# First stage of a transformer kernel: four row pieces, halved weight loads on two queues, and a later transpose

## The chip, the cores and the metric

The kernel runs on one core of one Trainium2 chip. The metric is the device time of one execution in microseconds (us), lower is better. A core has TensorE (PE, with its weight loads PEld), VectorE (DVE), ScalarE (ACT), GpSimd (POOL) and SyncE (SP); SP and ACT issue transfers here, each through a queue of its own (q1 is SP's, q10 is ACT's), and 16 DMA engines carry both.

## What is computed

The reference is a model of two blocks over 256 tokens of width 1024. Only the beginning of the first block matters here, the input product of the mLSTM mixer:

```
def mlstm_mixer(x, w_in, b_ig, b_fg, head_g, w_out):
    B, S, _ = x.shape
    proj = x @ w_in
    q, k, v, o, ig, fg = jnp.split(proj, M_SPLITS, axis=-1)
...
```

x is 256 x 1024 in float32 and w_in is 1024 x 3080. Everything else (the recurrent cell, attention, feed-forward layers, the second block) comes after this product.

## The kernel before

**Precision.** A float32 product is made of three matmuls on rounded parts. For the weights, ACT writes the high part `wh` from the landed float32 weights (`split_half_high`, L314) and DVE writes the low part `wl`, the difference (`split_half_low`, L324). For the rows, TensorE turns 128x128 tiles of x into PSUM (L3321), ACT copies the high part `xT_high` (L3444), DVE the low part `xT_low` (L3542). The products are high rows by high weights (wh,xT_high), low rows by high weights (wh,xT_low), and high rows by low weights (wl,xT_high).

**Tiling.** x has eight tiles of 128 columns; two neighbours form a *pair*, and the step `xturn pair` turns the four 128x128 blocks of one pair (two tiles, two groups of 128 rows). The weights come as numbered *loads* into a ring of four slots of 2048 columns. Loads 0 and 1 are the first 392 columns of w_in (in two strips, 8 columns and 384 columns), for the first and the last four tiles of x; loads 2 and 3 are the next 512 columns. Each load is split into a half 0 (two tiles) and a half 1. I write half (1,0) for half 0 of load 1.

**Order.** The first stage has one hand-written list, `steps()`. TensorE, ACT and DVE each walk the whole list in order and issue their own part of each step. So a step's place in the list fixes its place in three instruction streams, and each of these engines takes its stream in order. `dense c, half, t, ks` is TensorE's product for column group c, load 2c + half, row group t and tiles ks; `high n, j` is ACT's split and `low n, j` DVE's. An `xturn` is TensorE's four transposes, then ACT's copy of `xT_high`, then DVE's `xT_low`. In the dense step of c = 0, t = 0 the three kinds of product are taken in the order in which their operands come (L3284 wh,xT_high; L3287 wh,xT_low; L3290 wl,xT_high), each with its own wait; the step for t = 1 follows at L341 to L343. The list begins:

```
        yield "xturn", 0
        yield "high", 0, 0
        yield "low", 0, 0
        yield "xturn", 1
        yield "high", 0, 1
        yield "dense", 0, 0, 0, range(2)
        yield "dense", 0, 0, 1, range(2)
        yield "low", 0, 1
        yield "xturn", 2
        yield "xturn", 3
        yield "dense", 0, 0, 0, range(2, 4)
        yield "dense", 0, 0, 1, range(2, 4)
        yield "high", 1, 0
        yield "low", 1, 0
```

**Transfers.** ACT issues half (0,0) (L3437: 8 KB, then 384 KB). SP issues the left half of x (pairs 0 and 1, 512 KB), half (0,1) (8 and 384 KB), the right half of x, load 1 whole (16 and 768 KB), loads 2 and 3 (1024 KB each), and then many small vectors. While the first rows are under way TensorE does four matmuls on ones (L3265), and five short ones after pair 0 (L3326); their results are not used.

Of the kernel before, what the change touches and what calls it, by code (L numbers as in the profile page):

```python
# [27 lines left out]
P = 128  # L28
SEQ = 256
TT = SEQ // P  # L30
D = 1024
KT = D // P
BANK = 512
# [23 lines left out]
SLOTS = 4  # L57
# [163 lines left out]
def parts_of(K, n):  # L221

    if K.slot_of[n] is None:
        return K.early_high[:, :], K.early_low[:, :]
    return K.wh[:, K.slot_of[n], :], K.wl[:, K.slot_of[n], :]
# [14 lines left out]
def joined(slot, k, width):  # L240
    return slot[:, 0:k * width].rearrange("p (k n) -> p k n", k=k)


def pieces_in(K, n, slot):

    out, at = [], 0
    if isinstance(K.loads[n], Joined):
        whole = joined(slot, K.loads[n][0].shape[1], sum(p.shape[2] for p in K.loads[n]))
        for src in K.loads[n]:
            out.append(whole[:, :, at:at + src.shape[2]])  # L250
            at += src.shape[2]
        return out
    for src in K.loads[n]:
        k, w = src.shape[1], src.shape[2]
        out.append(slot[:, at:at + k * w].rearrange("p (k n) -> p k n", k=k))
        at += k * w
    return out
# [8 lines left out]
def load_weights(K, sp, n):  # L266

    if n < len(K.loads):
        for dst, src in zip(pieces_in(K, n, K.ring[:, n % SLOTS, :]), K.loads[n]):
            sp.dma_start(dst, src).then_inc(K.slot_loaded[n % SLOTS], 16)  # L270


def load_size(K, n):
    return sum(p.shape[1] * p.shape[2] for p in K.loads[n])
# [22 lines left out]
def half_of(w, j):  # L297

    if w <= SLOT * 3 // 4:
        return (0, w) if j == 1 else None  # L300
    return (j * w // 2, (j + 1) * w // 2)


def split_half_high(K, act, n, j):

    if n < len(K.loads) and half_of(load_size(K, n), j):
        lo, hi = half_of(load_size(K, n), j)
        if n == 0 and j == 0:
            act.wait_ge(K.first_loaded, 16 * len(K.loads[0]))
        elif n == 0 or lo == 0:  # L310
            act.wait_ge(K.slot_loaded[n % SLOTS], 16 * sum(len(K.loads[m]) for m in range(n % SLOTS, n + 1, SLOTS)))
            if K.part_after[n] is not None:
                act.wait_ge(K.load_used, K.part_after[n] + 1)
        K.nc.scalar.activation(parts_of(K, n)[0][:, lo:hi], K.ring[:, n % SLOTS, lo:hi], ACT.Copy).then_inc(  # L314
            K.high_ready, 2 if lo == 0 and j == 1 else 1)
# [42 lines left out]
def refill(K, sp, first, count):  # L358

    for n in range(first + AHEAD, first + AHEAD + count):  # L360
        if n < len(K.loads):
            sp.wait_ge(K.low_ready, 2 * n + 2)
            load_weights(K, sp, n + SLOTS)
# [331 lines left out]
class Tail:  # L695
# [121 lines left out]
    def act(self, act, own=None):  # L817

        K, nc = self.K, self.K.nc
        for step, *args in self.order():  # L820
            if step == "square":
                t, h = args
                s = slice(h * BANK, (h + 1) * BANK)
                self.rows(act, t, h)
                nc.scalar.activation(K.hid_flat[:, t, s], K.x[:, t, s], ACT.Square,
                                     accum_out=K.stat[:, t, h:h + 1]).then_inc(K.square_ready.sem, 1)
            elif step == "high":
                t, h = args
                act.wait_ge(K.turned.sem, self.turned0 + 2 * t + h + 1)
                for first, n in self.tiles(h):  # L830
                    m = nc.scalar.activation(K.xT[0][:, first:first + n, t * P:(t + 1) * P],
                                             self.bank(t, h, first, n), ACT.Copy, scale=self.scale(first))
                m.then_inc(K.high_turned.sem, 1)
            elif step == "lead_high":
                i, j = args
                if i == 0 and j == 0 and self.region:
                    act.wait_ge(*self.region)
                split_half_high(K, act, self.lead_load + i, j)
            elif own:
                own(step, *args)  # L840
# [470 lines left out]
def load_rows(K, sp, which):  # L1311

    for r, vec in which.items():
        w = vec.shape[0]
        sp.dma_start(K.rows[:, r, 0:w], vec.partition_broadcast(P)).then_inc(K.row_loaded[r], 16)
# [748 lines left out]
def nsa_mixer(K, a, tail):  # L2064
# [657 lines left out]
    def _(act):  # L2722
        for step, *args in steps():
            if step == "high":
                split_half_high(K, act, first + args[0], args[1])
            elif step == "take" and args[1] == 0:
                c, _ = args
# [292 lines left out]
def mlstm_mixer(K, a, tail):  # L3020
# [41 lines left out]
    def steps():  # L3062
# [7 lines left out]
        yield "dense", 0, 0, 1, range(2)  # L3070
        yield "low", 0, 1
        yield "xturn", 2
        yield "xturn", 3
        yield "dense", 0, 0, 0, range(2, 4)
        yield "dense", 0, 0, 1, range(2, 4)
        yield "high", 1, 0
        yield "low", 1, 0
        yield "high", 1, 1
        yield "low", 1, 1
# [151 lines left out]
    @block.sync  # L3231
    def _(sp):
        x_rows = a["x"][0].rearrange("(t p) d -> p t d", p=P)
        sp.dma_start(K.x[:, :, 0:BANK], x_rows[:, :, 0:BANK]).then_inc(K.input_loaded, 16)
        for dst, src in zip(pieces_in(K, 0, K.ring[:, 0, :]), K.loads[0]):
            sp.dma_start(dst[:, 2:4, :], src[:, 2:4, :]).then_inc(K.slot_loaded[0], 16)
        sp.dma_start(K.x[:, :, BANK:D], x_rows[:, :, BANK:D]).then_inc(K.rest_loaded, 16)
        for n in range(1, SLOTS):
            load_weights(K, sp, n)
        sp.dma_start(K.gate_bias[0:M_HEADS, 0:1], a["a_b_igate"][0].unsqueeze(1)).then_inc(K.bias_loaded, 16)  # L3240
        sp.dma_start(K.gate_bias[0:M_HEADS, 1:2], a["a_b_fgate"][0].unsqueeze(1)).then_inc(K.bias_loaded, 16)
        sp.dma_start(K.positions[:, :], a["positions"][0].rearrange("(t p) -> p t", p=P),
                      allow_slow_non_contiguous=True).then_inc(K.small_loaded, 16)
        for name, vec in lists:
            c, m = K.col_of[name], vec.shape[0] // P
            sp.dma_start(K.z[c:c + m, 0, 0:P], vec.rearrange("(k p) -> k p", p=P)).then_inc(K.small_loaded, 16)
        sp.dma_start(K.gate_bias[0:FOX, 2:3], a["b_forget_2"][0].unsqueeze(1)).then_inc(K.small_loaded, 16)
        sp.dma_start(K.sinks[:, :], a["b_sinks"][0].partition_broadcast(P)).then_inc(K.small_loaded, 16)
        refill(K, sp, first - AHEAD, 1)
        for i, name in enumerate(["q_norm_nsa_2", "k_norm_slc_2", "k_norm_win_2", "q_norm_fox_2", "k_norm_fox_2",  # L3250
                                  "k_norm_cmp_2"]):
            sp.dma_start(K.head_gain[:, i, :], a[name][0].partition_broadcast(P)).then_inc(K.small_loaded, 16)
        refill(K, sp, first - AHEAD + 1, 2)
        load_rows(K, sp, {0: a["mix_ln_g"][0], 1: a["mix_ln_b"][0]})
        refill(K, sp, first - AHEAD + 3, 11)
        sp.wait_ge(K.scores_ready.sem, H)
        load_rows(K, sp, {2: a["mlp_ln_g"][0], 3: a["mlp_ln_b"][0]})
        given.sp(sp)
        refill(K, sp, first - AHEAD + 14, 6)

    @block.tensor
    def _(pe):
        pe.wait_ge(K.ones_ready, 1)
        for i in range(4):
            nc.tensor.matmul(K.psum[:, 0, 0:SEQ], K.ones[:, 0:P], K.ones[:, :], start=True, stop=True)  # L3265
        for step, *args in steps():
            if step == "dense":
                c, half, t, ks = args
                n = first + 2 * c + half
# [40 lines left out]
                    mm.then_inc(K.filled.sem, 1)  # L3310
            elif step == "xturn":
                pair, = args
                if pair == 0:
                    pe.wait_ge(K.input_loaded, 16)
                    pe.wait_ge(K.masked, 1)
                elif pair == 2:
                    pe.wait_ge(K.rest_loaded, 16)
                for j in range(2):
                    for t in range(TT):
                        kk = 2 * pair + j  # L3320
# [113 lines left out]
    def _(act):  # L3434
        G = K.gates
        for dst, src in zip(pieces_in(K, 0, K.ring[:, 0, :]), K.loads[0]):
            act.dma_start(dst[:, 0:2, :], src[:, 0:2, :]).then_inc(K.first_loaded, 16)  # L3437
        for step, *args in steps():
            if step == "high":
                split_half_high(K, act, first + args[0], args[1])  # L3440
            elif step == "xturn":
                pair, = args
# [501 lines left out]
def build(nc, a, out):  # L3944
    K = Kit()
    K.nc = nc
    with ExitStack() as ctx:
# [3 lines left out]
        def sem(name):  # L3951
            return ctx.enter_context(nc.semaphore(name))
# [208 lines left out]
        K.high_ready = sem("high_ready")  # L4161
        K.low_ready = sem("low_ready")
        K.load_used = sem("load_used")
        K.input_loaded = sem("input_loaded")
        K.rest_loaded = sem("rest_loaded")
        K.first_loaded = sem("first_loaded")
        K.small_loaded = sem("small_loaded")
        K.bias_loaded = sem("bias_loaded")
        K.zeroed = sem("zeroed")
# [97 lines left out]
```

## Time and profile before

| | |
|---|---|
| median of 3 runs | 1200.76 us (1200.52 to 1201.33) |
| the profiled execution | 1200.72 us, of which span 1199.0 us |
| TensorE busy | 1186.3 us (99% of the span) |
| VectorE busy | 747.1 us (62%) |
| ScalarE busy | 618.9 us (52%) |
| bytes moved | 210.80 MB, mean 176 GB/s |

TensorE is busy almost without a gap. What matters is therefore the few places where it waits, and whether an edit makes one shorter or adds one. All of the edited code runs in the first 20 us of the span. In a row of the timeline, `x4` counts instructions merged into one row, and the square brackets hold how long the engine had been idle and what released it. A matmul's row on PE begins when its data streams; the weight load (PEld) of the same matmul begins somewhat earlier, and PEld rows are the better clock for "when did TensorE get here".

### The profile page before, as it was taken

To read this page: it belongs to the slowest core of one execution; us is meant where nothing else is said; L and a number is where in the kernel's file an instruction comes from. 1 tells how busy PE (TensorE), PEld (TensorE's weight loads), DVE (VectorE), ACT (ScalarE), POOL (GpSimd) and SP (SyncE) were. 2 spreads that over 40 slices of the span, in tenths; PEclk is the share of its full clock that TensorE was granted. 3 is DMA by queue.
4 is the path that set the end of the run, shared out by engine and by line. 5 is a ranking of instruction groups with operands and counts; after the bars stand their busy time and mean duration, and the time that the engine had idled before them with its cause. 6 is when DMAs were issued, how large, how long until landed. Compare 5 with 4: busy or idle time off the path is not lost.

```text
span 1199.0 us, 16307 instructions
## 1 busy us (share of the span) xinstructions
PE 1186.3 (99%) x6455; PEld 1009.3 (84%) x6455; DVE 747.1 (62%) x990; ACT 618.9 (52%) x924; POOL 42.5 (4%) x64
## 2 busy tenths in 40 slices
PE   9999999999999999999999999999999999999998
PEld 8888899898777789999888888888878788888887
DVE  6769655556865774554697455448986465554447
ACT  5464544344465544444456434436886674444445
POOL 2000000000000000000000000001111010000001
PEclk9999999999999999999999999999999999999999
DMA  8655554654753356556545565554651336655540
GB/s 292 209 188 207 194 194 163 206 197 153 228 180 111 115 210 198 189 177 202 184 145 187 194 209 178 182 171 144 192 166 69 115 124 210 195 191 171 180 176 36
DMA packets 119964, 210.80 MB, mean 176 GB/s; under 512 B 8320, under 2 KB 67024, under 8 KB 119888
## 3 DMA queue, kind: packets, MB, share of 16 engines
q1 hardware_dynamic: 119344, 209.35, 52.6%
q8 instruction: 52, 0.85, 0.3%
q10 hardware_dynamic: 544, 0.40, 0.1%
q14 instruction: 24, 0.20, 0.1%
HBM read 208.68 MB, written 1.05 MB: 175 GB/s over the span
## 4 chain that ended last, share of the span: by engine, by line
PE 90%; DVE 6%; ACT 2%; issue 1%; DMA 0%; POOL 0%; ACTq 0%; DVEq 0%; POOLq 0%
PE psum L341 23%; PE psum L343 23%; PE psum L342 23%; PE psum L349 4%; PE psum L355 3%; PE psum L350 3%; PE psum L1431 2%; PE psum L1399 2%; DVE wl L324 1%; PE psum L1418 1%; PE psum L853 1%; PE psum L540 1%; DVE early_low L324 1%; DVE bn L775 1%; DMA ring<-in_a_w_in 0%
## 5 line engine op out<-in xcount | busy, mean ns | idle before, releaser
L293 DVE TENSOR_TENSOR wl<-ring,wh 128x2048 fp32r<-128x2048 f32 x131 | 300.0, 2292 | 263.3 <-ACT wh L284 263.2
L284 ACT ACTIVATE wh<-ring 128x2048 fp32r<-128x2048 f32 x131 | 250.6, 1915 | 215.0 <-PE psum L343 215.0
L341 PE MATMUL psum<-wh,xT_high 128*128 128x512 f32 (+4 forms) x576 | 225.0, 391 | 0.0
L343 PE MATMUL psum<-wh,xT_low 128*128 128x512 f32 (+4 forms) x576 | 218.8, 380 | 0.0
L342 PE MATMUL psum<-wl,xT_high 128*128 128x512 f32 (+4 forms) x576 | 218.1, 379 | 0.0
L341 PE MATMUL psum<-wh,hidT_high 128*128 128x512 f32 (+2 forms) x472 | 178.8, 380 | 0.2
L342 PE MATMUL psum<-wl,hidT_high 128*128 128x512 f32 (+2 forms) x472 | 178.0, 379 | 0.0
L343 PE MATMUL psum<-wh,hidT_low 128*128 128x512 f32 (+2 forms) x472 | 177.9, 378 | 0.0
L341 PE MATMUL psum<-xT_high,wh 128*128 128x256 f32 x480 | 136.0, 283 | 0.0
L343 PE MATMUL psum<-xT_high,wl 128*128 128x256 f32 x480 | 135.8, 283 | 0.0
L342 PE MATMUL psum<-xT_low,wh 128*128 128x256 f32 x480 | 135.8, 283 | 0.0
L324 DVE TENSOR_TENSOR wl<-ring,wh 128x1024 fp32r<-128x1024 f32 (+4 forms) x101 | 120.8, 1214 | 11.5 <-ACT wh L314 10.9
L341 PEld LDWEIGHTS psum<-wh,xT_high 128*128 128x128 f32 x576 | 108.3, 188 | 20.5 <-issue 2.0
L343 PEld LDWEIGHTS psum<-wh,xT_low 128*128 128x128 f32 x576 | 108.3, 188 | 20.6
L342 PEld LDWEIGHTS psum<-wl,xT_high 128*128 128x128 f32 x576 | 108.5, 188 | 18.2
L314 ACT ACTIVATE wh<-ring 128x1024 fp32r<-128x1024 f32 (+4 forms) x101 | 103.2, 1057 | 34.6 <-PE psum L343 22.0
L341 PEld LDWEIGHTS psum<-wh,hidT_high 128*128 128x128 f32 (+2 forms) x472 | 85.3, 181 | 18.1 <-issue 1.4
L343 PEld LDWEIGHTS psum<-wh,hidT_low 128*128 128x128 f32 (+2 forms) x472 | 85.2, 181 | 17.4
L342 PEld LDWEIGHTS psum<-wl,hidT_high 128*128 128x128 f32 (+2 forms) x472 | 85.3, 181 | 16.6
L341 PEld LDWEIGHTS psum<-xT_high,wh 128*128 128x128 f32 x480 | 92.0, 192 | 0.6
L342 PEld LDWEIGHTS psum<-xT_low,wh 128*128 128x128 f32 x480 | 92.0, 192 | 0.6
L343 PEld LDWEIGHTS psum<-xT_high,wl 128*128 128x128 f32 x480 | 92.0, 192 | 0.0
(325 smaller groups left out, 1477.9 us busy)
## 6 DMA issues: line engine op xcount, KB each, us to landing
ring<-in_mlp_w_up SPq DMA_DIRECT2D x32, 1024.0 KB, 5.7
ring<-in_mlp_w_down SPq DMA_DIRECT2D x32, 1024.0 KB, 5.0
ring<-in_ffn_wg SPq DMA_DIRECT2D x44, 512.0 KB, 4.0
ring<-in_ffn_wu SPq DMA_DIRECT2D x44, 512.0 KB, 5.0
ring<-in_ffn_wd SPq DMA_DIRECT2D x22, 1024.0 KB, 5.0
ring<-in_ple_w_gate SPq DMA_DIRECT2D x12, 1024.0 KB, 5.1
ring<-in_w_in SPq DMA_DIRECT2D x10, 1024.0 KB, 5.1
ring<-in_a_w_in SPq DMA_DIRECT2D x8, 1024.0 KB, 10.5
```

What stands on the lines that cost most here:

```text
L284: K.nc.scalar.activation(parts_of(K, n)[0][:, 0:w], K.ring[:, n % SLOTS, 0:w], ACT.Copy).then_inc(K.high_ready, 2)
L293: K.nc.vector.tensor_tensor(low[:, 0:w], K.ring[:, n % SLOTS, 0:w], high[:, 0:w].bitcast(F32), ALU.subtract).then_inc(K.low_ready, 2)
L314: K.nc.scalar.activation(parts_of(K, n)[0][:, lo:hi], K.ring[:, n % SLOTS, lo:hi], ACT.Copy).then_inc(K.high_ready, 2 if lo == 0 and j == ...
L324: K.nc.vector.tensor_tensor(low[:, lo:hi], K.ring[:, n % SLOTS, lo:hi], high[:, lo:hi].bitcast(F32), ALU.subtract).then_inc(K.low_ready, 2 ...
L341: nc.tensor.matmul(out, x[0], w[0], start=start, stop=False)
L342: nc.tensor.matmul(out, x[0], w[1], start=False, stop=False)
L343: return nc.tensor.matmul(out, x[1], w[0], start=False, stop=stop)
L349: nc.tensor.matmul(out, x[0], w[0], start=start, stop=False)
L350: nc.tensor.matmul(out, x[0], w[1], start=False, stop=False)
L355: return K.nc.tensor.matmul(out, x[1], w[0], start=False, stop=stop)
L1399: nc.tensor.matmul(out, u["q"], u["k"], start=True, stop=False)
L1431: mm = nc.tensor.matmul(K.psum[:, self.value_bank, at:at + HD], self.probsT[:, i % 2, (2 * a + j) * P:(2 * a + j + 1) * P], u["v"][a][j], ...
```

## The change

x comes in four pieces of 256 columns (one per pair, 256 KB each), each with its own semaphore. Half (0,1) moves from SP's queue to ACT's, behind half (0,0). Load 1 comes in halves: half (1,0) goes on SP's queue between the third and the fourth piece of x, half (1,1) behind the fourth. One of the four matmuls on ones is gone. `xturn 3` stands behind `high 1, 0` in the list, and no longer in front of the products on tiles 2 and 3.

```
-        if n == 0 and j == 0:
-            act.wait_ge(K.first_loaded, 16 * len(K.loads[0]))
-        elif n == 0 or lo == 0:
+        if n <= 1 and j == 0:
+            act.wait_ge(K.first_loaded[n], 16 * len(K.loads[n]))
+        elif n <= 1 or lo == 0:
...
         yield "xturn", 2
-        yield "xturn", 3
         yield "dense", 0, 0, 0, range(2, 4)
         yield "dense", 0, 0, 1, range(2, 4)
         yield "high", 1, 0
+        yield "xturn", 3
         yield "low", 1, 0
...
-        sp.dma_start(K.x[:, :, 0:BANK], x_rows[:, :, 0:BANK]).then_inc(K.input_loaded, 16)
-        for dst, src in zip(pieces_in(K, 0, K.ring[:, 0, :]), K.loads[0]):
-            sp.dma_start(dst[:, 2:4, :], src[:, 2:4, :]).then_inc(K.slot_loaded[0], 16)
-        sp.dma_start(K.x[:, :, BANK:D], x_rows[:, :, BANK:D]).then_inc(K.rest_loaded, 16)
-        for n in range(1, SLOTS):
+        for pair in range(4):
+            s = slice(2 * P * pair, 2 * P * (pair + 1))
+            if pair == 3:
+                for dst, src in zip(pieces_in(K, 1, K.ring[:, 1, :]), K.loads[1]):
+                    sp.dma_start(dst[:, 0:2, :], src[:, 0:2, :]).then_inc(K.first_loaded[1], 16)
+            sp.dma_start(K.x[:, :, s], x_rows[:, :, s]).then_inc(K.input_loaded[pair], 16)
+        for dst, src in zip(pieces_in(K, 1, K.ring[:, 1, :]), K.loads[1]):
+            sp.dma_start(dst[:, 2:4, :], src[:, 2:4, :]).then_inc(K.slot_loaded[1], 16)
+        for n in range(2, SLOTS):
...
-        for i in range(4):
+        for i in range(3):
             nc.tensor.matmul(K.psum[:, 0, 0:SEQ], K.ones[:, 0:P], K.ones[:, :], start=True, stop=True)
...
-            act.dma_start(dst[:, 0:2, :], src[:, 0:2, :]).then_inc(K.first_loaded, 16)
+            act.dma_start(dst[:, 0:2, :], src[:, 0:2, :]).then_inc(K.first_loaded[0], 16)
+        for dst, src in zip(pieces_in(K, 0, K.ring[:, 0, :]), K.loads[0]):
+            act.dma_start(dst[:, 2:4, :], src[:, 2:4, :]).then_inc(K.slot_loaded[0], 16)
```

TensorE's stream, from the transposes of pair 2 on, before (eight transposes are pairs 2 and 3; the names after the arrow are the two operands):

```order
L3321 MATMUL psum<-ident,x 128x128 x8
L3284 MATMUL psum<-wh,xT_high 128x392 x2
L3287 MATMUL psum<-wh,xT_low 128x392 x2
L3290 MATMUL psum<-wl,xT_high 128x392 x2
L341 MATMUL psum<-wh,xT_high 128x392
L342 MATMUL psum<-wl,xT_high 128x392
L343 MATMUL psum<-wh,xT_low 128x392
L341 MATMUL psum<-wh,xT_high 128x392
L342 MATMUL psum<-wl,xT_high 128x392
L343 MATMUL psum<-wh,xT_low 128x392
L3284 MATMUL psum<-wh,xT_high 128x392 x2
```

and of the change at the same place:

```order
L3323 MATMUL psum<-ident,x 128x128 x4
L3288 MATMUL psum<-wh,xT_high 128x392 x2
L3291 MATMUL psum<-wh,xT_low 128x392 x2
L3294 MATMUL psum<-wl,xT_high 128x392 x2
L341 MATMUL psum<-wh,xT_high 128x392
L342 MATMUL psum<-wl,xT_high 128x392
L343 MATMUL psum<-wh,xT_low 128x392
L341 MATMUL psum<-wh,xT_high 128x392
L342 MATMUL psum<-wl,xT_high 128x392
L343 MATMUL psum<-wh,xT_low 128x392
L3323 MATMUL psum<-ident,x 128x128 x4
L3288 MATMUL psum<-wh,xT_high 128x392 x2
```

The four transposes of pair 3 have moved behind the twelve products of half (0,1), and stand directly ahead of the products of half (1,0).

DVE's stream of the change, from the first `xT_low` on (L3546 was L3542):

```order
L3546 TENSOR_TENSOR xT_low<-psum,xT_high 128x512 [waits input_high]
L324 TENSOR_TENSOR wl<-ring,wh 128x784 [waits high_ready]
L3546 TENSOR_TENSOR xT_low<-psum,xT_high 128x512 [waits input_high]
L324 TENSOR_TENSOR wl<-ring,wh 128x784 [waits high_ready]
L3546 TENSOR_TENSOR xT_low<-psum,xT_high 128x512 [waits input_high] x2
L324 TENSOR_TENSOR wl<-ring,wh 128x784 [waits high_ready] x2
L324 TENSOR_TENSOR wl<-ring,wh 128x1024 [waits high_ready] x4
```

Here nothing moved: both kernels have the same seven rows, `xT_low` of pairs 2 and 3 one behind the other and both ahead of the low parts of load 1.

ACT's stream before, from its first transfer on (each ACTIVATE to `wh` is one half of a load):

```order
L3437 DMA ring<-in_a_w_in 128x2x8
L3437 DMA ring<-in_a_w_in 128x2x384
L3444 ACT_TABLE_LOAD
L3444 ACTIVATE xT_high<-psum 128x512 [waits input_turned]
L314 ACTIVATE wh<-ring 128x784 [waits first_loaded]
L3444 ACTIVATE xT_high<-psum 128x512 [waits input_turned]
L314 ACTIVATE wh<-ring 128x784 [waits slot_loaded0]
L3444 ACTIVATE xT_high<-psum 128x512 [waits input_turned] x2
L314 ACTIVATE wh<-ring 128x784 [waits slot_loaded1]
L314 ACTIVATE wh<-ring 128x784
```

and of the change:

```order
L3439 DMA ring<-in_a_w_in 128x2x8
L3439 DMA ring<-in_a_w_in 128x2x384
L3441 DMA ring<-in_a_w_in 128x2x8
L3441 DMA ring<-in_a_w_in 128x2x384
L3448 ACTIVATE xT_high<-psum 128x512 [waits input_turned]
L314 ACTIVATE wh<-ring 128x784 [waits first_loaded0]
L3448 ACTIVATE xT_high<-psum 128x512 [waits input_turned]
L314 ACTIVATE wh<-ring 128x784 [waits slot_loaded0]
L3448 ACTIVATE xT_high<-psum 128x512 [waits input_turned]
L314 ACTIVATE wh<-ring 128x784 [waits first_loaded1]
L3448 ACTIVATE xT_high<-psum 128x512 [waits input_turned]
L314 ACTIVATE wh<-ring 128x784 [waits slot_loaded1]
```

ACT issues two more transfers, and now splits half (1,0) ahead of its copy for pair 3.

## Rows read from the trace of the kernel before

**Rows 1.** The page: busy time of each engine, and the chain's shares by engine.
```profile
PE 1186.3 (99%) x6455; PEld 1009.3 (84%) x6455; DVE 747.1 (62%) x990; ACT 618.9 (52%) x924; POOL 42.5 (4%) x64
...
PE 90%; DVE 6%; ACT 2%; issue 1%; DMA 0%; POOL 0%; ACTq 0%; DVEq 0%; POOLq 0%
```

**Rows 2.** The chain of waits, first 20 us: start us, us, what.
```profile
1.29 5.42 DMA ring<-in_a_w_in
6.73 0.86 ACT wh L314
```

**Rows 3.** Timeline of TensorE, first 18 us: start us, us, engine, line, instruction.
```profile
1.23 3.74 PE L3265 MATMUL psum<-ones 128*128 128x256 f32 x8 [1.23 <-DVE ones L3522]
...
4.94 0.42 PEld L3321 LDWEIGHTS psum<-ident,x 128*128 128x128 f32 x4 [0.64 <-DMA x<-in_x]
...
5.43 1.28 PE L3326 MATMUL psum<-ones 128*128 128x128 f32 x10
...
7.74 0.59 PE L3284 MATMUL psum<-wh,xT_high 128*128 128x392 f32 x2 [0.59 <-ACT wh L314]
...
8.65 0.30 PEld L3290 LDWEIGHTS psum<-wl,xT_high 128*128 128x128 f32 x2 [0.29 <-DVE wl L324]
...
10.01 0.98 PEld L3321 LDWEIGHTS psum<-ident,x 128*128 128x128 f32 x8
...
11.61 0.37 PEld L3290 LDWEIGHTS psum<-wl,xT_high 128*128 128x128 f32 x2
...
13.03 0.37 PEld L3284 LDWEIGHTS psum<-wh,xT_high 128*128 128x128 f32 x2
...
13.38 0.37 PEld L3287 LDWEIGHTS psum<-wh,xT_low 128*128 128x128 f32 x2
...
13.75 0.37 PEld L3290 LDWEIGHTS psum<-wl,xT_high 128*128 128x128 f32 x2
...
17.32 0.19 PEld L341 LDWEIGHTS psum<-xT_high,wh 128*128 128x128 f32 x1
```

**Rows 4.** Timeline of ACT, 7 to 13 us.
```profile
7.97 0.85 ACT L314 ACTIVATE wh<-ring 128x784 fp32r<-128x784 f32 x1
...
10.83 1.09 ACT L3444 ACTIVATE xT_high<-psum 128x512 fp32r<-128x512 f32 x2 [2.00 <-PE psum L3321]
...
11.80 1.61 ACT L314 ACTIVATE wh<-ring 128x784 fp32r<-128x784 f32 x2
```

**Rows 5.** Timeline of DVE, 7 to 17 us.
```profile
7.62 0.97 DVE L324 TENSOR_TENSOR wl<-ring,wh 128x784 fp32r<-128x784 f32 x1 [0.67 <-ACT wh L314]
8.52 0.69 DVE L3542 TENSOR_TENSOR xT_low<-psum,xT_high 128x512 fp32r<-128x512 f32 x1
9.12 0.97 DVE L324 TENSOR_TENSOR wl<-ring,wh 128x784 fp32r<-128x784 f32 x1
11.46 1.29 DVE L3542 TENSOR_TENSOR xT_low<-psum,xT_high 128x512 fp32r<-128x512 f32 x2 [1.37 <-ACT xT_high L3444]
...
12.69 1.86 DVE L324 TENSOR_TENSOR wl<-ring,wh 128x784 fp32r<-128x784 f32 x2
...
15.18 2.36 DVE L324 TENSOR_TENSOR wl<-ring,wh 128x1024 fp32r<-128x1024 f32 x2 [0.63 <-ACT wh L314]
```

**Rows 6.** Windows: busy of PE, PEld, DVE, ACT, POOL; clock, DMA share, GB/s.
```profile
0.00:6.00 6.00, 4.77 (x18) 3.59 (x19) 2.58 (x23) 1.65 (x2) 3.75 (x16) 1.00 0.58 169
6.00:8.00 2.00, 1.41 (x13) 1.20 (x12) 1.07 (x2) 1.49 (x4) 0.10 (x1) 1.00 1.07 397
8.00:10.00 2.00, 2.00 (x11) 1.71 (x11) 2.00 (x3) 0.82 (x2) 0.00 (x0) 1.00 1.11 364
```

**Rows 7.** DMA issues, first 60 us: count, KB, us from issue to landing.
```profile
x<-in_x SPq DMA_DIRECT2D x1, 512.0 KB, 4.1
...
ring<-in_a_w_in SPq DMA_DIRECT2D x1, 384.0 KB, 5.9
```

**Rows 8.** Timeline of TensorE, 80 to 100 us: its longest wait there.
```profile
85.44 0.66 PE L3404 MATMUL psum<-ident,z 128*128 128x128 f32 x4 [0.92 <-DVE z L3624]
```

More of the change, by code:

```diff
@@ L3312, in _ @@
                 pair, = args
+                pe.wait_ge(K.input_loaded[pair], 16)
                 if pair == 0:
-                    pe.wait_ge(K.input_loaded, 16)
                     pe.wait_ge(K.masked, 1)
-                elif pair == 2:
-                    pe.wait_ge(K.rest_loaded, 16)
                 for j in range(2):
@@ L4163, in build @@
         K.load_used = sem("load_used")
-        K.input_loaded = sem("input_loaded")
-        K.rest_loaded = sem("rest_loaded")
-        K.first_loaded = sem("first_loaded")
+        K.input_loaded = [sem(f"input_loaded{i}") for i in range(4)]
+        K.first_loaded = [sem(f"first_loaded{i}") for i in range(2)]
         K.small_loaded = sem("small_loaded")
```

## The prediction, made before the change was timed

> **What bounds the kernel now.** I read the page's busy shares first: TensorE is busy for 1186.3 of 1199.0 us, and the chain that ended last runs on it for 90% [rows 1]. So time appears or goes almost only where TensorE waits. All of the edits act in the first 20 us, so next I read the chain of waits there. It begins with a transfer and not with an engine: half (0,0) of the weights is issued at 1.29 and lands 5.42 us later, at 6.71; ACT splits it from 6.73 [rows 2]; TensorE, idle for 0.59 us, starts the first product at 7.74 [rows 3]. The timeline then gives TensorE's waits in the stretch: 0.64 us for the left half of x (until 4.94), 0.59 for `wh`, 0.29 for `wl` at 8.65 [rows 3]. Behind that it has no wait up to 17.32. The two waits that delay products are therefore worth 0.9 us together; the 0.64 delays nothing but transposes, which are long done when the weights land. That is the most that this stretch could give back.
>
> The reader should also see how near the operands come in. TensorE wants `wl` of half (1,0) at 13.75 [rows 3], and DVE begins to make it at 12.69 [rows 5]; one such split takes 0.97, so it is ready at 13.66. The margin is 0.09 us.
>
> **The change, part by part.** I write T for the moment at which TensorE has issued the last product of half (0,1). Before, that is PEld 13.03 [rows 3].
>
> *Matmul on ones removed.* The four are eight records over 3.74 us, 0.94 each [rows 3]. They end at 4.97 and overlap the wait for x, so removing one frees the engine at about 4.0, and rows or weights are still the ones waited for. Price 0. If this cover were gone, it would bring at most 0.94.
>
> *x in four pieces.* The 512 KB landed 4.1 us after their issue at 0.79, at 4.9 [rows 7]. A piece of 256 KB lands somewhere between 4.0 and 4.9. Pair 0 is turned up to 0.9 us sooner, and then ACT stands waiting for the weights as before. Price 0.
>
> *Start of the first product.* Half (0,0) has the same place on ACT's queue. By 6.0 us 6.0 x 169 GB/s = 1.01 MB had been moved [rows 6], and it landed 0.7 us after that. What SP's queue moves beside it decides: 0.52 MB if only pairs 0 and 1 go ahead of its end, 0.79 if all of the third piece does too. The sum with its own 0.40 is 0.93 to 1.19 MB, that is 0.3 us earlier to 0.45 later. Before, 0.61 MB of others went beside it, which lies between; I take 0, with -0.3 and +0.45 as bounds.
>
> *Half (0,1) on ACT's queue.* Before, it was SP's second transfer: issued at about 1.8, landed 5.9 later at 7.7 [rows 7], used by ACT from 7.97 [rows 4]. Now it is behind half (0,0). At its end ACT's queue has moved 0.80 MB. If SP's queue has moved as many packets by then, that is three pieces of x and 8 KB, 0.80 MB; if SP gets all up to the fourth piece through, 1.45 MB. The sum is 1.60 to 2.25 MB. With 1.01 MB at 6.0, 397 GB/s to 8.0 and 364 behind [rows 6] that is 7.5 to 9.2 us, and with 0.7 to 1.0 us until the landing shows, 8.2 to 10.2. I take 9.1, since SP's queue is ahead by then and has half (1,0) in hand: 1.4 us later than before. From its landing, `wl` is usable 1.92 later (ACT starts at 6.73, DVE at 7.62, TensorE at 8.65, rows of half (0,0)) [rows 2, 3, 5], at 11.0. TensorE wanted it at 11.61 [rows 3], and now wants it 0.49 earlier, because four transposes stand ahead of it and not eight (0.98 for eight): 11.12. So 0.1 us spare; hidden. A landing at 10.2 would cost 1.0 us. It decides from 9.2 on.
> The Trainium skill, page "DMA: Bandwidth & Descriptors", section "Issuing engines are not separate DMA queues", says that transfers started from several engines run on the same 16 DMA engines and interleave, and that issuing from two only saves issue time. By that, the second queue for half (0,1) brings no byte earlier and the term stays 0 at best; the trace agrees that the bytes are shared, 1.07 of the DMA engines' time being used from 6 to 8 us.
>
> *Pair 3 turned later.* This is the term that counts. On TensorE T comes 0.49 earlier by the transposes moved away, and they take the 0.49 back directly behind T: no gain. But what hung on them hangs on T now. DVE makes `xT_low` of pair 3 ahead of `wl` of half (1,0), in both kernels. Counted from the PEld start of the first transpose: ACT's copy starts 0.82 later (10.01 to 10.83) [rows 3, 4]; DVE's `xT_low` 0.63 behind it (10.83 to 11.46) [rows 4, 5]; DVE's next, `wl`, 0.60 behind that (8.52 to 9.12) [rows 5]; and TensorE has `wl` 1.03 after its start (7.62 to 8.65) [rows 5, 3]. Together 3.08 us. TensorE meanwhile has the transposes (0.49), two products with `wh`,`xT_high` (0.35) and two with `wh`,`xT_low` (0.37) [rows 3], 1.21 us, and stands at the third kind. **Wait: 3.08 - 1.21 = 1.87 us.** The `wh` of half (1,0) is not what is late: on SP's queue it ends at 0.80 (ACT's) + 0.79 + 0.40 = 1.99 MB, at 8.5, lands by 9.5, and is split before T.
>
> Queued behind that `wl` on DVE is `wl` of half (1,1). It takes 0.93 (1.86 for two, rows 5), while TensorE has three groups of two, 1.07: no second wait. Then come the halves of load 2: ready on DVE from 15.18 before, in both halves by 17.54 [rows 5]; later by the 2 us that DVE is late, 19.6. TensorE wanted the first half at 17.32 [rows 3] and is 1.87 late itself, 19.2, when the first half has been there for 0.8 us. No third wait. SP issues load 5 only when `wl` of half (1,1) is made; TensorE wants that load far later, as its own work on loads 1 to 4 lies ahead.
>
> *Is the delay given back?* Everything behind is fed by TensorE. Its longest wait in the next 100 us, 0.92 at 85.44 for DVE [rows 8], is for work that itself begins when TensorE ends its products; it moves along.
>
> **Sum.** Ones 0, x pieces 0, start 0, half (0,1) 0.1 (it stands 0.1 from where it decides, and the bounds are 0 and 1.0), pair 3 +1.87: 1200.72 + 1.97 = 1202.7 us. The profiled execution is within 0.04 of the median of the runs, so the same for that. What a measurement can tell from no change is 0.2%, 2.4 us: this forecast is slower by 0.16%, inside it.
>
> **The rivals.**
> *A. Slower beyond 0.2%, by half (0,1).* If its landing moves past 9.8, the wait for `wl` of half (0,1) exceeds 0.57, and 1200.72 + 1.87 + 0.57 reaches 1203.16. At the bound of 10.2 it gives 1.0: 1203.6; with the late start of 0.45 at most 1204.1. For it: 1.45 MB of SP's could go first. Against: queues that take turns let ACT's through sooner. The Trainium skill, same page, section "Queues, rings and completion order", says that each DMA engine goes round its queues packet by packet, which speaks for the early end. Chance 0.2.
> *B. The clock.* Eight records of 256 columns took 0.47 us each, ten of 128 columns 0.13 from 5.43 on [rows 3]: per column 1.8 ns and then 1.0 ns, the 1.2 and the 2.4 GHz level, though the window's row prints a granted clock of 1.00 [rows 6]. The engine had worked without pause from 1.23 before it rose. With one matmul fewer there is a gap before the first rows. If the rise came only behind pair 1, the ten records would take 1.2 us more and the transposes of pairs 0 and 1 (0.98 for eight) about as much again, some 0.8, less the 0.7 by which pair 0 may come sooner: pair 1 turned at about 8.4 in place of 7.1, and the first product 0.8 late: 1203.5. The 1.87 us wait could do the same later: the 18 products behind it at double price, 18 x 0.18 = 3.2 more, 1205.9. The Trainium skill, page "TensorE: Matmul & The Clock Gate", Part 1, says that the array runs at half clock until it has been kept busy and falls back when idle; no wait in these rows is as long as 1.87, so they cannot show it. Chance 0.08.
> *C. No delay.* The change does not cost what I say: the wait is shorter, as half (0,0) lands early and something later gives the rest back, or `wl` is made sooner than the program's order lets me believe. At best both product waits go, -0.9: 1199.8 to 1201.8. Against it stands that DVE takes its stream in order. Chance 0.11.
> My forecast (wait of 1.6 to 2.2 us, 1202.2 to 1203.1) has 0.61.
>
> **How the numbers follow.** Slower by over 0.2% holds A and B and a little of my own case's upper edge: 0.28. Faster by over 0.2% would need 2.4 us where the stretch can give 0.9 at most: 0.02, for something I don't see. The rest is 0.70. The range leaves out the strongest form of B and the better half of C: 1201.3 to 1204.1.
>
> **What would show it.** In the changed profile: PEld of the transposes of pair 3 at about 12.5; then a wait of TensorE for DVE's `wl` of 1.9 us ahead of L3294, at 15.6 in place of 13.75; `wl` rows of load 1 on DVE from 14.6; ACT idle about 1 us for pair 3's transposes; the first product of load 2 at about 19.2; first product near 7.7; half (0,1) split by ACT at about 9.1, 1.1 us later than before; the waits from 20 us on unchanged in size. I am wrong if no wait stands ahead of that L3294, if the first product starts more than 0.5 us away from 7.74, or if half (0,1) comes after 9.8.

## The result

The changed kernel takes 1202.62 us (median of 19 runs, 1202.41 to 1203.18) against 1200.66 us for the kernel before (19 runs, 1200.25 to 1201.33): ratio 1.0017, 95% interval 1.001 to 1.0023. It is 1.96 us slower; the forecast was 1202.7, or 1.97 slower. The interval of the ratio lies above 1, so the loss is real, and its middle is below the 0.2% that counts as a change here.

The page of the changed kernel, busy time of each engine, answers to [rows 1]; the span is 1201.1 us:

```profile
PE 1187.1 (99%) x6453; PEld 1010.2 (84%) x6453; DVE 746.7 (62%) x990; ACT 619.4 (52%) x924; POOL 42.5 (4%) x64
```

The shares say nothing about the loss. The timeline of TensorE's weight loads does; it answers to [rows 3]:

```profile
3.80 0.81 PEld L3323 LDWEIGHTS psum<-ident,x 128*128 128x128 f32 x4 [0.36 <-DMA x<-in_x]
4.59 2.26 PEld L3328 LDWEIGHTS psum<-ones 128*128 128x128 f32 x10
6.73 0.69 PEld L3323 LDWEIGHTS psum<-ident,x 128*128 128x128 f32 x4
7.88 0.30 PEld L3288 LDWEIGHTS psum<-wh,xT_high 128*128 128x128 f32 x2 [0.46 <-issue]
...
12.77 0.54 PEld L3323 LDWEIGHTS psum<-ident,x 128*128 128x128 f32 x4
13.27 0.30 PEld L3288 LDWEIGHTS psum<-wh,xT_high 128*128 128x128 f32 x2
13.56 0.36 PEld L3291 LDWEIGHTS psum<-wh,xT_low 128*128 128x128 f32 x2
15.84 0.30 PEld L3294 LDWEIGHTS psum<-wl,xT_high 128*128 128x128 f32 x2 [1.91 <-DVE wl L324]
```

The last row is the loss. TensorE has done the first two kinds of product of half (1,0) and then waits 1.91 us for DVE's `wl`. That product stood at 13.75 [rows 3] and stands at 15.84, 2.09 later; 0.18 of it was there from the first product on (7.70 for its weight load before, 7.88 now). The chain of waits between 12.7 and 16 us shows who holds it:

```profile
13.11 0.45 PE psum L3323 x4
13.56 0.02 issue
13.58 0.61 ACT xT_high L3448
14.19 0.02 issue
14.21 0.69 DVE xT_low L3546
14.90 0.89 DVE wl L324
15.79 0.04 issue
15.84 0.62 PE psum L3294 x2
```

Transposes of pair 3, ACT's copy, DVE's `xT_low`, and only then `wl` of half (1,0), which needs none of the three. ACT had made the `wh` for it long before, and DVE stood idle, as the timelines of ACT and DVE show (they answer to [rows 4, 5]):

```profile
11.49 0.85 ACT L314 ACTIVATE wh<-ring 128x784 fp32r<-128x784 f32 x1
13.58 0.60 ACT L3448 ACTIVATE xT_high<-psum 128x512 fp32r<-128x512 f32 x1 [1.24 <-PE psum L3323]
```

```profile
11.63 0.69 DVE L3546 TENSOR_TENSOR xT_low<-psum,xT_high 128x512 fp32r<-128x512 f32 x1 [0.70 <-ACT xT_high L3448]
14.21 0.69 DVE L3546 TENSOR_TENSOR xT_low<-psum,xT_high 128x512 fp32r<-128x512 f32 x1 [1.89 <-ACT xT_high L3448]
```

DVE idles 1.89 us ahead of the row at 14.21. The `wh` and the weights from which it could make `wl` of half (1,0) are there from 12.3 on (11.49 + 0.85 on ACT), but `xT_low` of pair 3 stands ahead of that in its stream. Behind 16 us the delay stays: the first product of load 2, at 17.32 before [rows 3], has its weight load at 19.35, and the wait that stood at 85.44 [rows 8] stands 2.03 us later, with the same size.

```profile
87.47 0.66 PE L3406 MATMUL psum<-ident,z 128*128 128x128 f32 x4 [0.92 <-DVE z L3628]
```

### The profile page after: what moved, and what is told of

It reads as the page before. It is cut to its first block, busy times and chain, and to the rows that moved or that the text cites. A ratio compares the mean times of both kernels' runs of the same rounds, so it can differ in the third digit from the quotient of the medians.

```text
span 1201.1 us, 16307 instructions
## 1 busy us (share of the span) xinstructions
PE 1187.1 (99%) x6453; PEld 1010.2 (84%) x6453; DVE 746.7 (62%) x990; ACT 619.4 (52%) x924; POOL 42.5 (4%) x64
## 4 chain that ended last, share of the span: by engine, by line
PE 89%; DVE 7%; ACT 2%; issue 1%; DMA 0%; POOL 0%; ACTq 0%; DVEq 0%; POOLq 0%
PE psum L341 23%; PE psum L343 23%; PE psum L342 23%; PE psum L349 4%; PE psum L355 3%; PE psum L350 3%; PE psum L1431 2%; PE psum L1399 2%; DVE wl L324 1%; PE psum L1418 1%; PE psum L853 1%; PE psum L540 1%; DVE early_low L324 1%; DVE bn L775 1%; DMA ring<-in_a_w_in 0%
```

## The experiments

The theory: the loss is the place of one step in the list. The moved transposes carry with them, on DVE, work that TensorE needs sooner. Rivals: the transfers (half (0,1) behind half (0,0), smaller pieces), and TensorE's clock after the missing matmul on ones. Each median below is of 11 runs, and each is set against 33 runs of the kernel before on the same chip. The 95% interval of each ratio reaches about 0.0009, or 1.1 us, to either side. So the medians alone do not tell differences of less than a microsecond apart, and the sizes are read from the waits in the traces (one profiled execution of each kernel).

### Only the turn moved

Kernel before, with this edit alone:

```
         yield "xturn", 2
-        yield "xturn", 3
         yield "dense", 0, 0, 0, range(2, 4)
         yield "dense", 0, 0, 1, range(2, 4)
         yield "high", 1, 0
+        yield "xturn", 3
         yield "low", 1, 0
```

> The kernel before with one edit: the fourth pair is turned behind the splitting step of half (1,0); transfers and ones as before. My theory (the moved transposes carry the low part of half (1,0) with them, since DVE takes its stream in order): TensorE waits 1.87 us at the third kind of product of half (1,0), which starts at PEld 15.6 in place of 13.75; 1200.7 + 1.87 = 1202.5 us, and everything from there on is 1.9 later. Rival (the loss comes from the transfers: half (0,1) later, pieces smaller): this kernel keeps the old transfers, so it stays at 1200.7 and has no such wait.

Measured: 1202.3 us against 1200.53, ratio 1.0016 (1.0008 to 1.0025): +1.8 us. The timeline of TensorE's weight loads of this kernel has the same wait:

```profile
13.41 0.37 PEld L3287 LDWEIGHTS psum<-wh,xT_low 128*128 128x128 f32 x2
15.68 0.30 PEld L3290 LDWEIGHTS psum<-wl,xT_high 128*128 128x128 f32 x2 [1.91 <-DVE wl L324]
```

One moved line in a list makes the same wait and, within the interval, the whole loss, with the old transfers and all four matmuls on ones.

### The turn moved back

Changed kernel, `xturn 3` directly behind `xturn 2` again.

> The changed kernel with one edit undone: the fourth pair is turned directly behind the third, as before; four pieces, two queues and three matmuls on ones stay. My theory: no wait at the third kind of product of half (1,0); what is left is the first product 0.18 us later, so 1200.8 to 1201.0 us; the fourth piece of x, landed at 10.65 in the changed kernel's trace, is wanted at 10.65, a wait of at most 0.2. Rival (transfers carry the loss): stays at 1202.6.

Measured: 1200.72 us against 1200.53, ratio 1.0002 (0.9993 to 1.001). The transfers and the ones together cost nothing that the runs can tell. The 0.18 us that I had carried over from the changed kernel's profile did not come back: the first weight load stands at 7.51, and the median lies a little below the 1200.8 to 1201.0 expected. Its timeline of weight loads shows eight transposes without a wait for the fourth piece of x, and the third kind of product of half (1,0) at 13.58 in place of 15.84:

```profile
9.81 1.01 PEld L3323 LDWEIGHTS psum<-ident,x 128*128 128x128 f32 x8
...
13.58 0.36 PEld L3294 LDWEIGHTS psum<-wl,xT_high 128*128 128x128 f32 x2
```

### A dose: the turn between the two row groups

Changed kernel, with

```
         yield "xturn", 2
         yield "dense", 0, 0, 0, range(2, 4)
-        yield "dense", 0, 0, 1, range(2, 4)
         yield "high", 1, 0
         yield "xturn", 3
+        yield "dense", 0, 0, 1, range(2, 4)
         yield "low", 1, 0
```

> The changed kernel with the fourth pair turned between the two row groups of half (0,1) (behind the six products of t = 0, ahead of the six of t = 1), 1.07 us earlier on TensorE. A dose: my theory says the low part comes 3.08 us after the first transpose, so the wait shrinks from 1.91 to about 0.85 and the time to 1202.6 - 1.06 = 1201.6 us. If the wait came from something that does not hang on the transposes (a transfer, ACT's split), it keeps its 1.9 us and the time 1202.6.

Measured: 1201.43 us against 1200.53, ratio 1.0008 (0.9999 to 1.0017). The interval still holds 1; the median lies where it was expected, and the reading rests on the wait in its timeline, 0.83 us, where 0.85 had been worked out:

```profile
11.45 0.54 PEld L3323 LDWEIGHTS psum<-ident,x 128*128 128x128 f32 x4
...
14.52 0.30 PEld L3294 LDWEIGHTS psum<-wl,xT_high 128*128 128x128 f32 x2 [0.83 <-DVE wl L324]
```

From the first transpose to the product it is 3.07 us here (11.45 to 14.52) and 3.07 in the changed kernel (12.77 to 15.84). The wait moves with the transposes; a transfer or ACT's split of half (1,0) would have kept it at 1.9 us.

### Only DVE's order mended

Changed kernel, with `xturn 3` behind `low 1, 0`: TensorE's and ACT's streams stay, and DVE makes `wl` of half (1,0) ahead of `xT_low` of pair 3.

> The changed kernel with the step of the fourth pair behind the low part of half (1,0) and not ahead of it: only DVE's stream changes, TensorE's and ACT's are the same. My theory: the wait of 1.91 us for the low part of half (1,0) goes, since DVE can make it from 12.35 on. A smaller wait comes in its place at half (1,1), whose high part stands on ACT behind the copy of pair 3: high part ready at 14.95, TensorE wants it at 14.3 (0.65), and the low part ready at about 15.95, wanted 15.65 (0.3). Third kind of product of half (1,1) at 16.0 in place of 16.84: 1202.6 - 0.85 = 1201.75 us. Rival (DVE's order is not what holds it): 1202.6, with the wait still ahead of the same product.

Measured: 1201.45 us against 1200.53, ratio 1.0007 (0.9998 to 1.0016), 1.2 below the changed kernel and 0.3 below what was expected. The waits account for 0.86 of the 1.2 (0.76 + 0.29 in place of 1.91); the profiled execution also had its first product 0.61 us sooner (7.27 against 7.88 for its weight load). In its timeline the big wait is gone and two smaller ones stand one half further on, as expected:

```profile
13.38 0.36 PEld L3294 LDWEIGHTS psum<-wl,xT_high 128*128 128x128 f32 x2
14.49 0.30 PEld L3288 LDWEIGHTS psum<-wh,xT_high 128*128 128x128 f32 x2 [0.76 <-issue]
...
15.44 0.30 PEld L3294 LDWEIGHTS psum<-wl,xT_high 128*128 128x128 f32 x2 [0.29 <-DVE wl L324]
```

These are ACT's `wh` of half (1,1), held behind ACT's copy of pair 3 (0.76, 0.65 expected), and the `wl` made from it (0.29, 0.3 expected). The same pattern, on the next engine.

### Both mended

Changed kernel, with the turn between the row groups and behind `low 1, 0`.

> The changed kernel with both repairs of the list: the fourth pair is turned between the two row groups of half (0,1), and stands behind the low part of half (1,0) on DVE. My theory: no wait of TensorE for load 1 at all. Low part of half (1,0) made from 12.05 on, usable 13.1, wanted 13.7; low part of half (1,1) at 14.65, wanted 14.75. What is left of the changed kernel is its transfers, whose first product came between 7.3 and 7.9 us, so 1200.3 to 1200.9 us: the time before. If only one of the two causes were real, a wait of 0.8 (1201.4) would stay.

Measured: 1200.51 us against 1200.44, ratio 1.0002 (0.9993 to 1.0011). No wait for load 1 is left in the timeline of weight loads:

```profile
11.29 0.53 PEld L3323 LDWEIGHTS psum<-ident,x 128*128 128x128 f32 x4
12.80 0.37 PEld L3288 LDWEIGHTS psum<-wh,xT_high 128*128 128x128 f32 x2
13.15 0.37 PEld L3291 LDWEIGHTS psum<-wh,xT_low 128*128 128x128 f32 x2
13.51 0.37 PEld L3294 LDWEIGHTS psum<-wl,xT_high 128*128 128x128 f32 x2
```

So pair 3 can be turned later without a loss that the runs can tell: `wl` of half (1,0) is put ahead of it on DVE, and it is turned early enough for half (1,1), which still stands behind it on both engines. Nor is it a gain.

### The matmul on ones, in both kernels

First the changed kernel with the fourth one back (`range(3)` to `range(4)`):

> The changed kernel with the fourth matmul on ones put back. In the changed kernel's profile the ten short ones records ran at half speed (2.26 us against 1.28 before) and the first product came 0.18 later. Theory: that slowness is hidden behind the weights' landing (transposes of pair 1 end at 7.4 to 7.7, the product cannot start before 7.9), so putting the matmul back changes nothing: 1202.6 us, 0.0 to 0.2 less, and the 1.9 us wait stays. Rival (the clock is part of the loss): 1202.4 or less, with the first product at 7.7.

Measured: 1202.49 us against 1200.44, ratio 1.0017 (1.0008 to 1.0026): as the changed kernel. The wait stayed at 1.90 us. But the edit did not bring the fast short records back in the profiled execution, so by itself it doesn't test the clock rival:

```profile
5.45 2.05 PEld L3328 LDWEIGHTS psum<-ones 128*128 128x128 f32 x10
```

What does answer the rival for the changed kernel is the distance from ACT's start on `wh` of half (0,0) to the weight load of the first product. It is 0.97 us in the profile of the kernel before (6.73 [rows 2] to 7.70) and 0.96 in that of the changed kernel (6.92 to 7.88), though the short records took 1.20 us in the first and 2.26 in the second. So the first product waited for the weights in both, and the slow stretch cost nothing there. In the run with four ones it is 1.14 (6.71 to 7.85), since TensorE had turned pair 1 only at 7.89: later rows (three of the transposes of pair 0 at 4.81) and slow short records together cost it 0.17.

Then the kernel before with the fourth one removed and nothing else:

> The kernel before with only the fourth matmul on ones removed. Rows land as before, at 4.9 to 5.3, so TensorE pauses about 1 us. Theory (price 0): 1200.6 us as before. Rival (the clock): the short records run at half speed up to the first product, pair 1 is turned at 8.3 in place of 7.2, the first product comes 0.6 later and 1201.2 us, with the short ones at 2.3 us in place of 1.3.

Measured: 1201.6 us against 1200.44, ratio 1.0008 (0.9999 to 1.0017). The interval holds 1, but the runs lie between 1200.2 and 1202.52, a spread of 2.3 us, where 33 runs of the kernel before lie within 0.7; seven of the eleven are at 1201.33 or above, and none of the 33 is above 1200.79. So most executions lose and four do not. The profiled one (1201.33) had this timeline of weight loads:

```profile
4.83 0.72 PEld L3321 LDWEIGHTS psum<-ident,x 128*128 128x128 f32 x4 [1.39 <-DMA x<-in_x]
5.53 2.26 PEld L3326 LDWEIGHTS psum<-ones 128*128 128x128 f32 x10
7.66 0.87 PEld L3321 LDWEIGHTS psum<-ident,x 128*128 128x128 f32 x4
8.52 0.45 PEld L3284 LDWEIGHTS psum<-wh,xT_high 128*128 128x128 f32 x2
```

In the profile of the kernel before, the short matmuls on ones are this row:

```profile
5.32 1.20 PEld L3326 LDWEIGHTS psum<-ones 128*128 128x128 f32 x10
```

With three ones TensorE's weight loads idled 1.39 us ahead of the rows, and the short ones took 2.26 us in place of 1.20, the 1.2 GHz level and not the 2.4 GHz one. The turning of pair 1 began 1.2 us late (7.66 in place of 6.44) and the first product's weights loaded at 8.52 in place of 7.70. ACT had started on `wh` at 6.48, so by the distance of 0.97 the product could have come at 7.45: the clock rival is real in this kernel and cost 1.07 us in this execution. In the changed kernel the rows come earlier (transposes at 3.80 in place of 4.94), which pays for the slow stretch: there the same 2.26 us ended with pair 1 turned at 7.42, 0.46 ahead of the first product's weight load. The median loss, 1.2 us, is larger than the 0.82 of the profiled run; no profile shows one of the slower executions, so what they lost beyond it stays open.

### The wide strip first

The kernel with both mended, with half (0,0) issued as 384 KB and then 8 KB:

```
-        for dst, src in zip(pieces_in(K, 0, K.ring[:, 0, :]), K.loads[0]):
+        for dst, src in reversed(list(zip(pieces_in(K, 0, K.ring[:, 0, :]), K.loads[0]))):
             act.dma_start(dst[:, 0:2, :], src[:, 0:2, :]).then_inc(K.first_loaded[0], 16)
```

> The kernel of the run between_low_first with the two pieces of half (0,0) issued in the other order: 384 KB first, 8 KB behind. Theory: the narrow piece (256 rows of 32 bytes) holds ACT's queue from 2.8 to about 4.0 us before the wide one flows, and behind the wide one it overlaps with it; half (0,0) lands 0.3 to 0.6 us sooner, the first product at 7.0 to 7.4, and 1200.1 to 1200.4 us, below the time before. Rival (bytes alone decide): no change against between_low_first. The first piece of x may land up to 0.5 later, at 4.7, which still lies ahead of the weights.

Measured: 1202.02 us against 1200.44, ratio 1.0012 (1.0003 to 1.0021); three of the eleven runs are at 1200.9 to 1201.0, the others at 1201.9 or above. My expectation fell. Its timeline of weight loads:

```profile
5.35 0.71 PEld L3323 LDWEIGHTS psum<-ident,x 128*128 128x128 f32 x4 [1.91 <-DMA x<-in_x]
6.05 2.26 PEld L3328 LDWEIGHTS psum<-ones 128*128 128x128 f32 x10
8.18 0.87 PEld L3323 LDWEIGHTS psum<-ident,x 128*128 128x128 f32 x4
9.03 0.55 PEld L3288 LDWEIGHTS psum<-wh,xT_high 128*128 128x128 f32 x2
```

With the wide strip beside it from the start, the first piece of x came at 5.35 and not at 3.9. TensorE idled 1.91 us, the clock stayed at its low level, and the first product came 1.5 us late. The transfers between 2.0 and 3.9 us show it, first of the kernel with both mended, then of this one (q1 is SP's queue, with the rows; packets, MB, share of 16 engines):

```profile
q1 hardware_dynamic: 426, 0.42, 67.3%
q10 hardware_dynamic: 297, 0.05, 17.3%
```

```profile
q10 hardware_dynamic: 97, 0.15, 52.1%
q1 hardware_dynamic: 215, 0.22, 41.9%
```

SP's queue moved 0.42 MB beside the narrow strip and 0.22 MB beside the wide one. The narrow strip ahead was not a hindrance but let x through.

### The first half over both queues

The kernel with both mended; tile 0 of half (0,0) goes on ACT's queue, tile 1 on SP's behind the first piece of x, and pair 1 is turned behind the products of t = 0 on pair 0:

```
-        yield "xturn", 1
-        yield "high", 0, 1
         yield "dense", 0, 0, 0, range(2)
-        yield "dense", 0, 0, 1, range(2)
+        yield "high", 0, 1
         yield "low", 0, 1
+        yield "xturn", 1
+        yield "dense", 0, 0, 1, range(2)
```

> The kernel of the run between_low_first, with half (0,0) split over both queues (tile 0 on ACT's, tile 1 on SP's behind the first piece of x) and pair 1 turned behind the six products of t = 0. The first product then needs only 0.26 MB of x and 0.40 MB of weights. Theory: what sets the first product is the bytes ahead of it on both queues, about 0.86 MB in place of 1.01, so half (0,0) lands at 6.1 to 6.3 in place of 6.5, the first product at 7.1 to 7.3; half (0,1) behind it lands at 7.5 to 8.5, ahead of its need; 1200.0 to 1200.3 us, 0.2 to 0.4 below the time before. Rival: half (0,1) or pair 1 comes too late for the earlier start, or the first piece of x lands late and TensorE's clock stays low: 1200.5 or more.

Measured: 1200.81 us against 1200.56, ratio 1.0003 (0.9994 to 1.0012): no gain, and my expectation of 1200.0 to 1200.3 fell. The transfers did what was expected. The weights of the first product came 0.2 sooner than with both mended (ACT splits them at 6.29 and not at 6.51), and the first product's weight load stood at 7.26, against 7.48. Its timeline of weight loads:

```profile
7.26 0.30 PEld L3291 LDWEIGHTS psum<-wh,xT_high 128*128 128x128 f32 x2 [1.30 <-issue]
...
8.58 0.45 PEld L3326 LDWEIGHTS psum<-ident,x 128*128 128x128 f32 x4
...
11.52 0.54 PEld L3326 LDWEIGHTS psum<-ident,x 128*128 128x128 f32 x4
```

The transposes of pair 1, at 8.58, now stand between products. Before, they were done while TensorE waited for the weights anyway. They cost 0.45 and the earlier start brought 0.22, so at the transposes of pair 3 (11.52 against 11.29) this kernel is 0.23 us behind the one with both mended. I had not counted them. No variant tried here beats the kernel before.

## Why the prediction was right

**The wait.** Worked out 3.08 - 1.21 = 1.87 us; measured 1.91. The four steps were 0.82, 0.63, 0.60 and 1.03; they measured 0.81 (12.77 to 13.58), 0.63 (13.58 to 14.21), 0.61 (14.21 to 14.82, by the start of DVE's `wl` row) and 1.02, 3.07 together. The small miss is in TensorE's own work meanwhile: it took 1.15 (12.77 to the end of the weight loads of L3291 at 13.92) and not 1.21, since the first two products directly behind transposes took 0.29 (13.27 to 13.56) and not the 0.35 taken from a place behind products. The order of the list is shown as the cause by the edit alone (+1.8), by its undoing (+0.2), by the dose (0.83 for 0.85) and by mending DVE's order.

**The start.** Taken as 0, between -0.3 and +0.45. The changed kernel's profile has +0.18. Four variants with the same transfers and three ones (turn back, between, low first, both) had their first weight load at 7.51, 7.58, 7.27 and 7.48, and that of the kernel before, in its timeline, stands at 7.70:

```profile
7.70 0.30 PEld L3284 LDWEIGHTS psum<-wh,xT_high 128*128 128x128 f32 x2 [0.80 <-issue]
```

So the +0.18 belongs to that execution, whose half (0,0) landed that much later: ACT starts on it at 6.92, against 6.73 before. 0 was a fair value, but the lower bound was too narrow, as 7.27 is 0.43 earlier. The medians show no gain from the earlier starts.

**Half (0,1).** ACT was forecast to split it at 9.1 and did at 9.06:

```profile
6.92 0.86 ACT L314 ACTIVATE wh<-ring 128x784 fp32r<-128x784 f32 x1 [1.27 <-DMA ring<-in_a_w_in]
...
9.06 0.86 ACT L314 ACTIVATE wh<-ring 128x784 fp32r<-128x784 f32 x1 [0.76 <-DMA ring<-in_a_w_in]
```

The 0.1 us to spare was close to the middle of what came. In the changed kernel's profile `wl` is usable at 10.98 (its start at 9.95 and the 1.03 of the prediction) and wanted at 11.34, so 0.36 was spare, half of it from the late first product. Where pair 3 is turned late and the first product came earlier, nothing was: 0.00 in the kernel with both mended, and gaps of 0.12 and 0.11 in the runs between and low first. With the fourth matmul on ones put back (split at 9.44) the wait for it was 0.22. So the 0.1 that the sum charges for this half was not paid in the changed kernel. Rival A needed a landing past 9.8; none of the profiles had one.

**The sum.** In the profiles it came as 0.18 for the start, 0 for half (0,1) and 1.91 for the wait, 2.09 in all, against 0, 0.1 and 1.87. That the medians differ by 1.96, within 0.01 of the forecast 1.97, is partly luck. Two slips in the working changed nothing: the margin of 0.09 us for `wl` of half (1,0) before is 0.03 by the 1.03 that the prediction uses itself further on, and rivals A and B make up the 0.28 for "slower" alone, so that nothing of it is left for the forecast's own upper edge.

**Ones.** "Price 0" was right for this change and its working was incomplete. It looked for a gain only, up to 0.94, and treated the cost in rival B. The kernel before with the same removal lost 1.2 us in the median. What hid it in the changed kernel was, by the timelines, the earlier first piece of x, to which I had given the price 0 as well: with three ones, the kernels with rows at 4.83 and 5.35 had the weight load of their first product at 8.52 and 9.03, those with rows at 3.8 to 4.2 at 7.26 to 7.88. The two edits belong together.

**Behind 20 us.** Nothing given back and nothing added: 2.09 us late at 15.84, 2.03 at 19.35 and at 87.47, and spans 2.1 apart.

**Rivals.** B's slow stretch came, in the changed kernel too (2.26 us for the short ones), without B's price. B had the first product 0.8 us late with rows 0.7 sooner and pair 1 turned at 8.4; the rows came 1.14 sooner, pair 1 was turned at 7.42, and the weights were still what the product waited for. The wait of 1.91 us did not lower the clock: the products behind it stand 0.36 us per two (16.12, 16.48, 16.84), as before. C is out, since the wait came in full.

## What to carry to other kernels

Where several engines walk one list in order, moving a step moves it in every stream: look at what stands behind it on each engine, and whether that work needs the moved step at all. Work that TensorE does while it waits anyway is free where it stands and costs its full length once moved in between products. Whether a filler matmul ahead of the first operands is worth its place depends on when the operands land: taking one of four away cost 1.2 us in the median where the rows came at 4.8 us, and nothing that the runs can tell where they came at 3.8.

## What the hardware showed that I had not expected

**The rise of TensorE's clock is not fixed in time.** The ten short records on ones stand behind identical code in the changed kernel and in the variants turn back, between, low first and both. Their weight loads took 2.26, 1.69, 1.43, 1.20 and 1.46 us. Ahead of the rows its weight loads had paused 0.36, 0.33, 0.44, 0.79 and 0.47 us. The longest of these pauses stands ahead of the fastest records. In other kernels of this case four matmuls on ones and pauses of 0.64 and 1.02 us (the kernel before, only the turn moved) stand ahead of 1.20, four with no pause above 0.20 (the fourth put back) ahead of 2.05, and three with 1.39 and 1.91 (three ones in the kernel before, the wide strip first) ahead of 2.26. So neither the number of fillers nor the length of the pause puts these profiles in order; what does stays open. The granted clock printed for these stretches is 1.00 all the same; the 1.2 and the 2.4 GHz level are seen in the durations alone.

**Two queues do not share alike.** With a narrow strip (256 rows of 32 bytes) ahead on ACT's queue, SP's first piece of x (256 KB) was there at 3.8 to 4.2 us in five profiles; with a strip of 1536-byte rows ahead, at 5.35 in one. Bytes also move more slowly at the start. The 169 GB/s over the first 6 us [rows 6] hold 2 us in which almost nothing moves, but the rest is still below the 397 behind it. The same windows, cut finer:

```profile
0.00:2.00 2.00, 0.77 (x2) 0.68 (x3) 0.93 (x3) 0.17 (x1) 0.48 (x5) 1.00 0.02 6
2.00:6.00 4.00, 4.00 (x18) 2.91 (x17) 1.65 (x21) 1.48 (x2) 3.27 (x11) 1.00 0.86 250
```

Whether it is the size of the rows or their number in front that decides was not tried.
